# A two-block transformer kernel on one core: gates and branch products turned token-major and dealt out between compress and attention steps

## The reference

```python
h = rms_norm(x, attn_pre_gain)
u = h @ w_in                      # q, k, v of two attentions, nsa gates, g_a, g_b
o_a = swa_sink_attention(qa, ka, va, attn_sinks)
kc = compress(kcb, ...); vc = compress(vcb, ...)   # gelu(flat @ w1 + b1) @ w2, 15 blocks of 32 tokens
o_b = nsa_attention(...)          # compressed, selected and window branch, 8 heads of 64
mixed = jax.nn.sigmoid(g_a) * (o_a @ w_branch_a) + jax.nn.sigmoid(g_b) * (o_b @ w_branch_b)
x = x + rms_norm(mixed @ w_out, attn_post_gain)
x = x + rms_norm(conv_ffn(rms_norm(x, ffn_pre_gain), ...), ffn_post_gain)
```

## Time and profile before

| | us |
|---|---|
| median of 3 runs | 1836.22 |
| lowest and highest | 1832.48, 1836.95 |
| the profiled execution | 1835.49 |
| its span, first to last instruction | 1833.6 |
| mean granted TensorE clock | 0.984 |
| PE, PEld, DVE, ACT, POOL busy, share of span | 97%, 82%, 67%, 57%, 36% |
| chain that ended last: PE, ACT, DVE | 94%, 3%, 2% |

### The profile page before, as it was taken

The page is one execution under the profiler, slowest core; times in us unless marked ns, Lnnn a source line. Parts: engine busy times, 40 slices in busy tenths (PEclk is TensorE's granted clock), DMA queues, the critical chain, the costliest instruction groups (busy, mean ns, idle before and its releaser), DMA issues.

```text
span 1833.6 us, 26407 instructions
## 1 busy us (share of the span) xinstructions
PE 1770.3 (97%) x9874; PEld 1498.3 (82%) x9874; DVE 1224.4 (67%) x1924; ACT 1052.6 (57%) x1988; POOL 661.7 (36%) x656
## 2 busy tenths in 40 slices
PE   5989999999989999999999999999999999999998
PEld 5865888888865888888888887888888888778887
DVE  6855689975765689976665644766476657356663
ACT  5567576665477576655555556655465536565543
POOL 3114316620113326622662012566046600306640
PEclk9979999999989999999999999999999999899999
DMA  8731566665631566675766561765666575327661
GB/s 233 194 99 29 179 171 191 176 222 169 159 109 46 162 184 184 176 234 164 203 177 218 172 196 47 205 186 180 210 184 184 173 240 189 111 70 207 188 210 72
DMA packets 412224, 307.22 MB, mean 168 GB/s; under 512 B 10083, under 2 KB 366773, under 8 KB 412097
## 3 DMA queue, kind: packets, MB, share of 16 engines
q1 hardware_dynamic: 411312, 304.82, 56.5%
q0 software_dynamic: 784, 0.72, 0.2%
HBM read 304.45 MB, written 1.05 MB: 167 GB/s over the span
## 4 chain that ended last, share of the span: by engine, by line
PE 94%; ACT 3%; DVE 2%; issue 1%; DMA 1%; SPq 0%; POOL 0%; DVEq 0%; ACTq 0%
PE bank L1295 34%; PE bank L1296 17%; PE bank L1367 8%; PE bank L1368 8%; PE bank L1369 8%; PE bank L1345 3%; PE bank L1346 3%; PE bank L1335 3%; PE bank L1511 2%; PE bank L1493 1%; PE bank L1482 1%; DMA raw<-in_w_in 1%; ACT whi L511 1%; PE bank L1568 1%; ACT hsA L511 1%
## 5 line engine op out<-in xcount | busy, mean ns | idle before, releaser
L1295 PE MATMUL bank<-hsA,whi 128*128 128x512 f32 x2496 | 891.9, 402 | 2.1 <-DVE TA L823 2.1
L815 DVE TENSOR_TENSOR wlo<-raw,whi 128x1024 fp32r<-128x1024 f32 (+1 forms) x568 | 726.4, 1304 | 201.9 <-ACT whi L511 198.1
L1296 PE MATMUL bank<-hsA,wlo 128*128 128x256 f32 x2496 | 703.5, 282 | 0.0
L511 ACT ACTIVATE whi<-raw 128x1024 fp32r<-128x1024 f32 (+1 forms) x568 | 571.1, 1033 | 132.1 <-PE bank L1369 98.2
L1295 PEld LDWEIGHTS bank<-hsA,whi 128*128 128x128 f32 x2496 | 472.6, 189 | 120.0 <-DVE wlo L815 3.2
L1296 PEld LDWEIGHTS bank<-hsA,wlo 128*128 128x128 f32 x2496 | 474.8, 190 | 0.2
L511 ACT ACTIVATE low<-bank 128x256 f32<-128x256 f32 (+1 forms) x404 | 151.0, 377 | 367.9 <-PE bank L1296 330.4
L1179 POOL TENSOR_TENSOR HB<-CB,UB 128x256 f32<-128x256 f32 x88 | 123.7, 1406 | 363.7 <-ACT CB L514 363.1
L1367 PE MATMUL bank<-whi,hid 128*128 128x512 f32 x528 | 206.0, 390 | 0.0
L1369 PE MATMUL bank<-wlo,hid 128*128 128x512 f32 x528 | 205.6, 389 | 0.0
L1368 PE MATMUL bank<-whi,hid 128*128 128x512 f32 x528 | 205.4, 389 | 0.0
(11 more groups left out here) (217 smaller groups left out, 2014.2 us busy)
## 6 DMA issues: line engine op xcount, KB each, us to landing
raw<-in_ffn_w_up SPq DMA_DIRECT2D x176, 512.0 KB, 5.2
raw<-in_ffn_w_down SPq DMA_DIRECT2D x120, 512.0 KB, 4.5
raw<-in_w_in SPq DMA_DIRECT2D x104, 512.0 KB, 5.9
raw<-in_ffn_w_gate SPq DMA_DIRECT2D x88, 512.0 KB, 4.0
raw<-in_w_out SPq DMA_DIRECT2D x32, 512.0 KB, 4.5
raw<-in_ffn_w_down SPq DMA_DIRECT2D x24, 256.0 KB, 3.0
G<-in_norm_g SPq DMA_DIRECT2D x12, 512.0 KB, 7.5
raw<-in_cmp_w SPq DMA_DIRECT2D x8, 512.0 KB, 5.3
```

What stands on the lines that cost most here:

```text
L511: return nc.scalar.activation(out_, in_, func, **kw)
L815: v.tensor_tensor(wlo[c_ % RING][:, x:y], raw[:, c_ % RAW, x:y], whi[c_ % RING][:, x:y].bitcast(F32), ALU.subtract)\
L1295: mm(bank[b][:, 0:2 * n], whi[slot][:, at:at + P], rhs[:, 0:2 * n], start=x == 0, stop=False, **g32)
L1296: ins = mm(bank[b][:, n:2 * n], wlo[slot][:, at:at + P], rhs[:, 0:n], start=False, stop=x == len(ks) - 1, **g32)
```

## The change

1. `tile` orders its products high, low, low, high, high, low, ... instead of high, low, high, low. All wide tiles of all blocks are made by it.
2. The gates are token-major: 4 groups of 16 steps (`gate_step`), each step 3 products of 512 columns, 192 products in a layer for the 8 wide chunks before. A group fills two banks (128 tokens each), which DVE copies out (`gate_evict`, 8 copies of 128x512).
3. Steps 0 to 31 stand after the w_in chunks. From product 8 on, one compress product follows each gate product, 64 in all; key and value of compress come before step 26 (KV_STEP), z before step 28 (Z_STEP), and then the softmax of compress is waited for.
4. Steps 32 to 63 are dealt to the turns of attention: one behind the scores, and in every even turn one more ahead of the value products.
5. Attention has six banks: scores 1, 3, 4, 5, transposes 6 alone, outputs 2 alone. So transposes of map m wait for `pt_out` of map m - 1 (before: m - 2), and value products of a unit for `o_done` of the unit before (before: two before). Value products are issued once for the even heads into partitions 0 to 63 and once for the odd into 64 to 127, each with half the columns. The copies to hsB become one operation on 128 partitions, and DVE's stands ahead of its reciprocals.
6. The splits of five chunks (ten halves) are placed in turns 2, 3, 5, 6, 9, 10, 13, 14, 20, 21 of attention on ACT and DVE (SPLITS), and four copies of gates on DVE (EVICT). Before, no split stood in attention.
7. The branch products are token-major: 4 chunks of 24 products of 512 columns, 96 for the 64 pairs before. DVE multiplies with the gates from PSUM and adds; 16 transposes (`mixed_rows`) bring the sum back, and ACT and DVE split it. POOL has no part in it any more.
8. Loads of gates and branches read rows of 512 columns instead of 128 and 256.

```diff
+GATE_STEPS, CMP_AT, KV_STEP, Z_STEP = 64, 8, 26, 28
+EVICT = {5: 4, 11: 5, 16: 6, 21: 7}
+SPLITS = {2: (0, 0), 3: (0, 1), 5: (1, 0), 6: (1, 1), 9: (2, 0), 10: (2, 1), 13: (3, 0), 14: (3, 1), 20: (4, 0), 21: (4, 1)}
...
             for x, (at, rhs) in enumerate(ks):
-                mm(bank[b][:, 0:2 * n], whi[slot][:, at:at + P], rhs[:, 0:2 * n], start=x == 0, stop=False, **g32)
-                ins = mm(bank[b][:, n:2 * n], wlo[slot][:, at:at + P], rhs[:, 0:n], start=False, stop=x == len(ks) - 1, **g32)
+
+                def high():
+                    return mm(bank[b][:, 0:2 * n], whi[slot][:, at:at + P], rhs[:, 0:2 * n], start=x == 0, stop=False, **g32)
+
+                def lower():
+                    return mm(bank[b][:, n:2 * n], wlo[slot][:, at:at + P], rhs[:, 0:n], start=False, stop=False, **g32)
+                if x % 2:
+                    lower()
+                    ins = high()
+                else:
+                    high()
+                    ins = lower()
...
+            def gate_product(s, x):
+
+                grp, q, kk = p["gates"][s // 16], s % 16 // 4, s % 4
+                x_, th = grp["quarters"][q]
+                c, k, u = grp["c"] + x_, 4 * x_ + kk, s // 16 * 2 + th
+                y, slot = bank[GATE_BANK[s // 16][th]][:, :], (grp["c"] + x_) % RING
...
+                hi, lo = hsA[:, k, th * P:th * P + P], hsA[:, k, S + th * P:S + th * P + P]
+                ins = mm(y, lo if x == 1 else hi, (wlo if x == 2 else whi)[slot][:, kk * HALF:kk * HALF + HALF],
+                         start=k == 0 and x == 0, stop=k == KD - 1 and x == 2, **g32)
...
+                for x in range(3):
+                    gate_product(s, x)
+                    if 0 <= 3 * s + x - CMP_AT < 64:
+                        cmp_product(3 * s + x - CMP_AT)
             pe.wait_ge(cmp_p, L + 1)
...
                     ins.then_inc(scores_ready, 1)
+                if s < GATE_STEPS:
+                    gate_step(s)
+                    s += 1
                 m = i - SKEW
                 if 0 <= m < len(MAPS):
...
-                    if m >= 2:
-                        pe.wait_ge(pt_out, done + m - 1)
+                    if m:
+                        pe.wait_ge(pt_out, done + m)
...
+                if i % 2 == 0 and s < GATE_STEPS:
+                    gate_step(s)
+                    s += 1
                 m = i - SKEW - 1
...
-                    if br < 2 and o >= 2:
-                        pe.wait_ge(o_done, 12 * L + o - 1)
...
+                    if br < 2 and o:
+                        pe.wait_ge(o_done, 12 * L + o)
...
+                    for e in range(2):
+                        O = bank[2][HD * e:HD * e + HD, 0:n // 2]
+                        if br == 1:
+                            x0 = (hs[0] - 4 * g) * P
+                            mm(O, VC[0:N_CMP, g, :], every_other(PCT[0:N_CMP, 2 * g + qb, x0:x0 + n], e), start=True, stop=False, **g32)
+                        for kb in range(qb + 1):
+                            ins = mm(O, V1[:, br, kb, HD * g:HD * g + HD], every_other(PT[:, m % 2, kb * n:kb * n + n], e),
+                                     start=br == 0 and kb == 0, stop=br != 1 and kb == qb, **g32)
...
+                if i in EVICT:
+                    gate_evict(EVICT[i])
+                if i in SPLITS:
+                    x, part = SPLITS[i]
+                    split_to(p["gates"][3]["c"] + x, part)
...
+            def gated(q):
+                for th in range(2):
+                    u = 4 * q["dh"] + 2 * q["b"] + th
+                    src = branch_bank(q["dh"], q["b"], th)[:, :]
+                    dve.wait_ge(sg_ready, 8 * L + u + 1)
+                    dve.wait_ge(pass_done, q["halves"][th])
+                    if q["b"] == 0:
+                        seq.link(v.tensor_tensor(TA[:, th, :], src, gate_place(u), ALU.mult))
+                    else:
+                        m_ = M[:, th, half(q["dh"])]
+                        seq.link(v.tensor_tensor(m_, src, gate_place(u), ALU.mult))
+                        v.tensor_tensor(m_, m_, TA[:, th, :], ALU.add).then_inc(mix_ready, 1)
```

More of the change, by code:

```diff
@@ L75, in host_constants @@
     return c
-EARLY = 3
-BRANCH = [("mix", 0), ("gate", 3), ("mix", 1), ("gate", 4), ("gate", 5), ("mix", 2), ("gate", 6), ("gate", 7), ("mix", 3)]
 SKEW = 3
+GATE_STEPS, CMP_AT, KV_STEP, Z_STEP = 64, 8, 26, 28
 class Plan:
     def __init__(self):
-        self.chunks, self.tiles, self.passes = 0, 0, 0
+        self.chunks, self.tiles, self.passes, self.compressed = 0, 0, 0, 0
         self.size, self.free = [], []
@@ L202, in build @@
     KC = sb("KC", [P, 30])[0]
-    VC = [sb(f"VC{L}", [16, 2, HD], at=low_at + 4 * S * ((PLAN.one[L]["early"][2][1] + 2) % 4))[0] for L in range(DEPTH)]
     H = sb("H", [P, 2, D], at=hsB_at)[0]
@@ L304, in slot_free @@
             kind, n = PLAN.free[c - RING]
-            eng.wait_ge(sum_ready if kind == "sum" else pass_done, n)
+            eng.wait_ge({"sum": sum_ready, "pass": pass_done, "cmp": cmp_sum}[kind], n)
     def y_bank(th, dh):
@@ L1396, in _, with swaps_and_values @@
             n0, t0 = 2 * L, p["in"][0][1]
[L1397 to L1416 removed]
+            def swaps_and_values(c):
                 for t in (2 * c - 2, 2 * c - 1):
@@ new lines, in gate_step, with cmp_product @@
+            def gate_step(s):
+                for x in range(3):
+                    gate_product(s, x)
+            def cmp_product(i):
+                n, k, part = i // 32, i % 32 // 2, i % 2
+                c = p["cmp"][n]
+                if k == 0 and part == 0:
+                    chunk_here(c)
+                    pe.wait_ge(cmp_rhs, 2 * L + n + 1)
+                    pe.wait_ge(gates_ready, L + 1)
+                    pe.wait_ge(swap_used, 11 * L + 11 if n else 11 * L + 10)
+                b, w_ = bank[4 + n], (wlo if part else whi)[c % RING][:, k * P:k * P + P]
+                if part:
+                    ins = mm(b[:, 30:60], w_, RH[:, n, k, 0:30], start=False, stop=k == 15, **g32)
+                else:
+                    ins = mm(b[:, 0:60], w_, RH[:, n, k, :], start=k == 0, stop=False, **g32)
+                if k == 15 and part:
+                    ins.then_inc(cmp_sum, 1)
@@ new lines, in _ @@
+            pe.wait_ge(gate_out, 8 * L + 8)
+            for q in p["branch"]:
+                c = q["c"]
+                chunk_here(c)
+                if q["dh"] and q["b"]:
+                    for th in range(2):
+                        mixed_rows(0, th)
+                for th in range(2):
+                    y = branch_bank(q["dh"], q["b"], th)[:, :]
+                    for k in range(4):
+                        hi, lo = hsB[:, 4 * q["b"] + k, th * P:th * P + P], hsB[:, 4 * q["b"] + k, S + th * P:S + th * P + P]
+                        cols = slice(k * HALF, k * HALF + HALF)
+                        mm(y, hi, whi[c % RING][:, cols], start=k == 0, stop=False, **g32)
+                        mm(y, lo, whi[c % RING][:, cols], start=False, stop=False, **g32)
+                        ins = mm(y, hi, wlo[c % RING][:, cols], start=False, stop=k == 3, **g32)
+                    ins.then_inc(pass_done, 1)
```

484 lines of the change are left out of this document (261 added, 223 removed).

## The result

| | before | after |
|---|---|---|
| median, us | 1836.22 | 1845.16 |
| lowest and highest | 1832.48, 1837.7 | 1844.68, 1850.16 |
| profiled execution, its span | 1835.49, 1833.6 | 1845.16, 1843.4 |
| mean granted clock | 0.984 | 0.983 |
| ratio to before, 95% interval | | 1.0056, 1.0039 to 1.0072 |

The changed kernel is slower by 8.9 us in the median (7 to 13 by the interval) and by 9.8 in the span of the profiled execution. Predicted were 1830, with 1811 to 1848 as the range, so the time lies in the range and the sign is wrong: 5.5 us faster was forecast.

A forecast was written before the change was run, and what follows sets the result against it. PE was taken as the bound (94% of the chain). A layer: 124.6 - 3.3 + 2.1 + 1.1 + 14.9 + 1 = 140.4, two 280.8 against 281.1; with wide tiles -5.2, 1835.5 became 1830 us, range 1811 to 1848.

The forecast's parts named there:

- For a low clock after such waits I add 1.: Attention: low clock following PE's waits was put at 1 us a layer.
- the stretches: First blocks, first gate chunk through attention to the first w_out product: 280.8 us in two layers, against 281.1 before.
- Rival 3: Attention: splits cost 25 us or the clock falls to 0.78; +10 us a layer, 1850 us; chance 0.20.
- the 88 that I had named as the sign of being wrong: Attention: about 78 us expected; under 70 or over 88 us would show the prediction wrong.
- The waits: Attention: new splits make PE wait 12.8 us over the turns plus 2.1 at the end, 14.9 a layer; bounds 4 and 25.
- PE has as much to do as before: Changed part of a layer: PE's own work 124.6 us after, 124.1 before (+0.5), before the value halves' gain.
- Low clock gone from the first stretch: First gate chunk to attention: clock of 0.78 and 0.86 rises near 1.0, wide products standing between narrow ones.
- Value halves side by side: Attention: even and odd value products overlap, saving 3.3 us a layer; ends 0 and 5.2.
- Wide tiles -5.2: Wide pairs outside the first blocks' w_up: fewer size changes save 5.2 us; ends 0 and 7.1.
- Rival 2: Attention: ACT and DVE run ahead, splits cost PE 4 instead of 14.9 us a layer; 1810 us; chance 0.22.
- rival 1: Value halves in strict order, or compress and tiles give nothing: +6.6 or +5.2, 1836 us; chance 0.22 shared with another rival.

The follow-up runs named there:

- even turns (2): Changed kernel with the ten halves dealt one to every second turn of attention (2, 4, .. 20) instead of in pairs: 1826.0 us, ratio 0.9949.
- kept clear (5): Changed kernel with chunk 0 split ahead of attention and the other eight halves in turns 1, 3, 10, 12, 14, 16, 18, 20: 1817.0 us, ratio 0.9903.
- DVE's half later (6): Changed kernel with its own turns for the halves, but DVE takes each half one turn after ACT's: 1801.9 us, ratio 0.9820.
- both (7): Changed kernel with the halves in every second turn and DVE's half one turn later than ACT's: 1801.7 us, ratio 0.9823.
- experiment 9: Changed kernel with DVE's halves one turn later and the 64 compress products in one block behind gate step 13: 1817.2 us, ratio 0.9906.
- experiment 8: Changed kernel with DVE's halves one turn later and the wide pairs in their old order: 1813.6 us, ratio 0.9881.
- experiments 3 and 4: Changed kernel without gate steps in attention, eight halves and gate copies moved ahead: 1835.4 us with six banks; the same with eight banks 1807.4 us.

## Why the prediction was wrong

The forecast was 5.5 us faster and the kernel became 8.9 slower. The accounts of attention in layer 0, from the windows and the waits: waits of PE, half of the time at 1.2 GHz (what it costs where PE is what counts), and the rest, which is PE's own work.

| kernel | attention | waits | low clock | own work |
|---|---|---|---|---|
| forecast | 78.6 | 14.9 | (1) | 63.7 |
| changed | 84.7 | 12.9 | 8.5 | 63.3 |
| even turns (2) | 78.2 | 9.6 | 5.1 | 63.5 |
| kept clear (5) | 70.1 | 7.0 | 0 | 63.1 |
| DVE's half later (6) | 67.9 | 3.6 | 0 | 64.3 |
| both (7) | 66.9 | 2.7 | 0 | 64.2 |

The forecast's own work is 44.0 + 1.2 - 3.3 + 32 steps of 0.68; the 1 stood outside its 78.6. In layer 1 the changed kernel has 86.1 = 13.6 + 10.2 + 62.3, the one kept clear 73.2 = 7.0 + 3.4 + 62.8, and the kernel of 6 67.9 = 3.4 + 0 + 64.5.

- **The step that failed: "For a low clock after such waits I add 1."** It measured 8.5 us in layer 0 and 10.2 in layer 1, and 1.7 more in each behind attention (24.4 us at 0.93, 22.8 at 1.00 in the kernel of 6): 22 us in the two layers, where 2 were put, without a row behind the 1. That is more than the whole miss of the stretches, 295.6 - 280.8 = 14.8. The stretch had the profile's own warning: 0.93 before, with waits of 1.9, 1.4, 1.3 and 0.8 us. Rival 3 spelt the mechanism out, and I had given it 0.20. Its sums don't hold together: 17.6 us a layer for a clock of 0.78 is 16.6 over the 1, not +10. Nor does its limit: it wanted waits of about 18 us a layer for a slower kernel, and the kernel was slower with 12.9 and 13.6. Attention at 84.7 and 86.1 us also lies under the 88 that I had named as the sign of being wrong.
- **The waits were right, and I took them as given.** In the order of the turns: turn 5 4.4 (4.9 forecast), turn 6 none (1.6), turn 7 1.8 (2.1), turns 9 and 10 1.7 (1.9), turn 14 2.3 (2.3), the end 1.8 (2.1), and 0.9 at the start that I had not. Their cause was in the prediction too, ACT's and DVE's half one behind the other, and experiment 6 shows that it is most of it: put DVE's half a turn behind ACT's and the waits fall from 12.9 to 3.6 us, and the low clock goes.
- **PE has as much to do as before: right.** Own work in attention stayed within 62.3 to 64.5 in both layers, for 63.7 forecast, whatever the waits. Gate steps in attention are not free filling; they take their 0.68 us each, as forecast.
- **Low clock gone from the first stretch: right**, and for the reason given (experiment 9).
- **Value halves side by side: right.** Two rows of the changed kernel, one unit with eight rows of 128 columns and the scores that follow:

```profile
149.27 0.67 PE L1643 MATMUL bank<-PT,V 128*64 128x128 f32 x8
149.86 0.48 PE L1604 MATMUL bank<-U,QR 64*128 64x256 f32 x1
```

  0.59 us from start to start, where the earlier trace rows have 1.01. The eight rows start in pairs, 0.01 us apart (149.27 and 149.28, then 149.43 and 149.44). By TensorEngine Tiling (Array Packing), Key Properties, in the Trainium skill, different tiles multiply in parallel, and the trace agrees. By the same skill's TensorE: Matmul & The Clock Gate, Part 3, matmuls start strictly in program order; with all even heads ahead of the odd ones in the program that would have left about 1.0 us by the forecast's estimate, and the trace differs. The rows don't say which half each belongs to; that a pair is one product of each half is inferred from the starts.
- **Wide tiles -5.2: 7.3 by stages** (experiment 8). The order saved 1.5 us on the 304 pairs of a w_up stage of the second blocks, 0.005 a pair for the 0.0032 forecast; the pair went from 0.353 to 0.349 us. In the first blocks w_up gave 1.3 us although DVE is busy throughout, and w_down took 1.3 back, 1.0 of it a wait for DVE's `wlo`: nothing, as forecast.
- **Rival 2, 1810**, held that ACT and DVE run ahead and the splits cost PE 4 instead of 14.9 us. With DVE's half one turn later that is what happens, at 3.6 us and 1801.9. Of rival 1, the strict order of the value halves is out.
- **Not seen: what six banks cost.** The prediction charged them only through the splits. Without filling they cost 13 us a layer (experiments 3 and 4); the sum has no term for it.

What stays open: that waits bring the clock down in the changed kernel rests on kernels in which both fell together; no run took away the one and left the other. A wait does not do it each time: a wait of 1.76 us in layer 0 of the changed kernel has no low clock behind it, and the same waits of up to 3.0 us in experiment 5 have none in layer 0 and 6.8 us in layer 1. What decides between these is not shown.

The parts as kernels, each on top of the one above: before 1834.8; order of pairs -13.7; value halves -5.6; token-major gates and branches with compress between them, eight banks -8.4; filling on six banks, DVE's half later -5.5, at 1801.9. DVE's half in ACT's turn instead: +43.3. Some of these differences are small beside the spread: the kernel with eight banks ran from 1805.4 to 1816.4, so the 8.4 and the 5.5 are good to about 4 us, and the 13.7 holds some 7 of tiles and the rest of clock.

## What to carry to other kernels

When one engine's piece of work is handed on to a second in the same turn of a pipeline, the second stands for all that the first has queued ahead, and everything queued behind it on the second waits too; give the second its piece a turn later before judging the schedule. Where PE is the bound, price a wait in a stretch of short products at up to its double: the low clock behind the waits cost from nothing (7.0 us of waits, experiment 5, layer 0) to nearly as much again (13.6 us of waits, 11.9 of clock, changed kernel, layer 1). A filling that needs banks of its own is to be weighed against the kernel that keeps the banks, not against the one that lacks both.

## What the runs showed of the hardware

- The clock came down during or behind waits of PE of 1.7 to 4.1 us among short products, though not at each of them (experiment 5), and also where PE didn't wait at all but ran 64 products of 30 and 60 columns in a row (experiment 9, 13.7 us at 1.2 GHz in each layer). Interleaved with products of 512 columns the same products ran at 2.4 GHz.
- GpSimd's 48 products in attention took 19.64 us in the changed kernel and 27.25 with DVE's half one turn later, where eight of them stand beside one of DVE's subtractions of two SBUF operands each. These eight took 1.28 to 1.53 us, where none took more than 0.48 in the changed kernel, while the subtraction kept its 1.22:

```profile
L1289 POOL TENSOR_SCALAR PB<-PB,st x48: 361/480/1532, 123.4 to 178.7; 128x128 f32<-128x128 f32 x24, 128x256 f32<-128x256 f32 x24
```

  The excess is 0.9 to 1.1 us for each of the eight, a little less than one subtraction. SBUF — State Buffer, SBUF: two separate sides, in the Trainium skill, describes a port pair that GpSimd and a VectorE instruction with two SBUF inputs take in turn, each for a whole instruction; the trace agrees. None of PE's waits in this attention is put down to GpSimd.
- A stretch at 1.2 GHz in the attention of a second block, worth 4 to 6 us, comes and goes between executions of the same kernel. With it the tile order's worth came out between 0 and 14 us, where the stages give 7.3.
